# A two-block transformer kernel: four of a head's sixteen expert value rows are weighted and added by VectorE instead of TensorE

## What is computed

```
q = (xt @ w_pq).reshape(T, PEER_HEADS, 2, PEER_QDIM // 2)      # T = 256 tokens, 8 heads
s = einsum('thpd,hpnd->thpn', q, subkeys)
top_s, top_i = lax.top_k(s, 16)                                 # per head and half
...                                                             # 16 best of the 16 x 16 sums
expert = take_along_axis(cand_i, best_pos); gate = softmax(best_s)
act = gelu(einsum('thkd,td->thk', peer_u[expert], x)) * gate    # 16 u rows per head and token
out = einsum('thk,thkd->td', act, peer_v[expert])               # 16 v rows per head and token
x = x + out
```

## Time and profile before

| | |
|---|---|
| timed runs | 1973.23 us median of 3 (1970.73 to 1973.85) |
| profiled execution | span 2142.0 us, 8.6% above the median; no time of its own is given beside the span |
| busy in that span | PE 80%, PE weight loads 51%, DVE 59%, POOL 47%, ACT 29% |
| granted PE clock | 0.88 of full speed, mean |
| DMA | 644.22 MB, mean 301 GB/s; 536.94 MB of it are the 1024 gathers |

### The profile page before, as it was taken

How to read it: one execution, slowest core, us unless ns; L and a number is a source line. 1 busy time by engine, 2 the same in 40 slices (tenths; PEclk the granted TensorE clock), 3 DMA queues, 4 the chain that set the end, 5 groups by cost and what they waited for, 6 DMA issues and landing times. The chain is left out here.

```text
span 2142.0 us, 22067 instructions
## 1 busy us (share of the span) xinstructions
PE 1722.3 (80%) x7643; PEld 1082.0 (51%) x7643; DVE 1254.5 (59%) x2789; ACT 616.9 (29%) x1151; POOL 1008.5 (47%) x1095
## 2 busy tenths in 40 slices
PE   8999999978787686768668999877777867677768
PEld 7998898844443232323224999754442322222323
DVE  6544665885565665566453456685555566476553
ACT  4472644412121111222213455312212111212212
POOL 3021000366666666667672000265666666666663
PEclk9998999989998787878778999898997878788878
DMA  7521553999999999999997756598999999999996
GB/s 253 165 82 60 172 188 116 307 365 341 347 371 373 351 367 383 352 366 368 361 391 241 232 161 197 187 338 332 342 367 375 361 364 370 365 372 370 359 376 240
DMA packets 243719, 644.22 MB, mean 301 GB/s; under 512 B 19541, under 2 KB 105354, under 8 KB 243610
## 3 DMA queue, kind: packets, MB, share of 16 engines
q0 software_dynamic: 147456, 536.94, 66.3%
q1 hardware_dynamic: 96154, 105.88, 15.4%
HBM read 641.69 MB, written 1.05 MB: 300 GB/s over the span
## 5 line engine op out<-in xcount | busy, mean ns | idle before, releaser
L2038 DVE SCALAR_TENSOR_TENSOR ex_uj<-wring,ps 128x1024 f32<-128x1024 f32 x496 | 601.8, 1219 | 409.7 <-DMA wring<-in_peer_u,ex_idx 363.7
L2334 PE MATMUL ps<-ex_v,ex_diag 128*128 128x512 f32 x1328 | 664.6, 647 | 168.4 <-issue 162.6
L2196 POOL DMA_INDIRECT wring<-in_peer_u,ex_idx x496 | 468.6, 945 | 176.1 <-issue 141.4
L2334 PEld LDWEIGHTS ps<-ex_v,ex_diag 128*128 128x128 f32 x1328 | 270.6, 206 | 546.2 <-issue 535.0
L2334 PE MATMUL ps<-value_rows,ex_diag 128*128 128x512 f32 x664 | 360.0, 677 | 135.4 <-issue 134.0
L2211 POOL DMA_INDIRECT ex_v<-in_peer_v,ex_idx x336 | 318.1, 947 | 242.3 <-remote 110.8
L2162 ACT ACTIVATE ex_diag<-ident,ex_weight 128x128 f32<-128x128 f32 x500 | 171.0, 393 | 720.0 <-remote 390.1
L2334 PEld LDWEIGHTS ps<-value_rows,ex_diag 128*128 128x128 f32 x664 | 141.7, 215 | 351.0 <-issue 345.4
L208 DVE TENSOR_TENSOR w_lo<-wring,w_hi 128x1024 fp32r<-128x1024 f32 (+1 forms) x160 | 187.3, 1211 | 108.4 <-ACT w_hi L199 106.1
L2196 POOL DMA_INDIRECT ex_v<-in_peer_u,ex_idx x16 | 16.4, 1023 | 464.1 <-PE ps L283 459.9
L2211 POOL DMA_INDIRECT value_rows<-in_peer_v,ex_idx x172 | 164.2, 955 | 96.3 <-remote 47.2
(11 more groups left out here) (470 smaller groups left out, 2465.0 us busy)
## 6 DMA issues: line engine op xcount, KB each, us to landing
wring<-in_w_in SPq DMA_DIRECT2D x42, 1024.0 KB, 5.4
wring<-in_w_ckv SPq DMA_DIRECT2D x8, 1024.0 KB, 5.3
wring<-in_peer_u,ex_idx POOLq DMA_INDIRECT x496
ex_v<-in_peer_v,ex_idx POOLq DMA_INDIRECT x336
wring<-in_w_mix_out SPq DMA_DIRECT2D x4, 1024.0 KB, 6.6
wring<-in_w_cq SPq DMA_DIRECT2D x4, 1024.0 KB, 5.1
wring<-in_w_co SPq DMA_DIRECT2D x4, 1024.0 KB, 5.2
value_rows<-in_w_pq SPq DMA_DIRECT2D x4, 1024.0 KB, 10.3
```

What stands on the lines that cost most here:

```text
L2038: ve.scalar_tensor_tensor(out=uj[i % 2], in0=u_row(i), scalar=1.0, in1=tokens(g // PH), op0=ALU.mult, op1=ALU.mult, accum_out=hidden[:, g ...
L2196: nc.gpsimd.indirect_dma_start(u_row(i), None, table_u, bass.IndirectOffsetOnAxis(ap=idx[:, g // PH, i % PER_T:i % PER_T + 1], axis=0)).th ...
L2334: last = mm(ps[:, 2 * T + c, :], diag[:, n % DIAGS, :], value_slot(v_slot(j))[:, c * BANK:(c + 1) * BANK], start=j % PER_T == 0, stop=ends)
```

## The change

`VEC_ROWS = {1: 2, 3: 6, 7: 10, 11: 14}`: in heads 0 to 14 of both stages, rows 2, 6, 10 and 14 of a head leave PE and ACT (no diagonal, no matmul). DVE handles them in the next head's loop, behind its u rows 1, 3, 7 and 11 and ahead of the top-k part there: it multiplies the row with its weight column and adds it to the residual tile, with both large operands in SBUF. The last head keeps its six. The slot of such a row is released by `vec_used`, and counts of semaphores are adjusted.

```
+VEC_ROWS = {1: 2, 3: 6, 7: 10, 11: 14}
...
         def on_vector(j):
-            return j >= FIRST_LAST and j - FIRST_LAST in LAST_VEC
+            return j - FIRST_LAST in LAST_VEC if j >= FIRST_LAST else j % TOPK in VEC_ROWS.values()
+
+        def before_on_vector(j):
+            return sum(1 for i in range(j) if on_vector(i))
 
         def on_tensor(j):
-            return j if j < FIRST_LAST else FIRST_LAST + sum(1 for i in range(FIRST_LAST, j) if not on_vector(i))
+            return j - before_on_vector(j)
+
+        VECTOR_ROWS = before_on_vector(ROWS)
+
+        def value_row(v, j):
+
+            T, g = j // PER_T, j // TOPK
+            v_arrived(v, j)
+            n = before_on_vector(j)
+            if n:
+                v.wait_ge(vec_used.sem, vec_used.at(n))
+            nc.vector.scalar_tensor_tensor(out=K.X[:, T, :], in0=value_slot(v_slot(j)), scalar=weight[:, g % 2, j % TOPK:j % TOPK + 1],
+                                           in1=K.X[:, T, :], op0=ALU.mult, op1=ALU.add).then_inc(vec_used.sem, 1)
...
                 if g >= 2:
-                    v.wait_ge(dia.sem, dia.at(TOPK * (g - 1)))
+                    v.wait_ge(dia.sem, dia.at(on_tensor(TOPK * (g - 1))))
...
                                             op0=ALU.mult, op1=ALU.mult, accum_out=hidden[:, g % 2, s:s + 1]).then_inc(u_used.sem, 1)
+                    if g and s in VEC_ROWS:
+                        if s == min(VEC_ROWS):
+                            v.wait_ge(wts.sem, wts.at(g))
+                        value_row(v, (g - 1) * TOPK + VEC_ROWS[s])
...
                 elif v_use(j):
-                    pool.wait_ge(pe_used.sem, pe_used.at(max(m for m in range(j) if slots[m] == n) + 1))
+                    m = max(m for m in range(j) if slots[m] == n)
+                    if on_vector(m):
+                        pool.wait_ge(vec_used.sem, vec_used.at(before_on_vector(m) + 1))
+                    else:
+                        pool.wait_ge(pe_used.sem, pe_used.at(on_tensor(m) + 1))
```

More of the change, by code:

```diff
@@ L1847, in _ @@
                     if n == RAW - 1:
-                        sp.wait_ge(pe_used.sem, pe_used.at(ROWS - len(LAST_VEC)))
-                        sp.wait_ge(vec_used.sem, vec_used.at(len(LAST_VEC)))
+                        sp.wait_ge(pe_used.sem, pe_used.at(ROWS - VECTOR_ROWS))
+                        sp.wait_ge(vec_used.sem, vec_used.at(VECTOR_ROWS))
                     K.load_unit(sp)
@@ L2057, in _ @@
                     first_low(n - len(LAST_VEC) + 3)
[L2058 to L2063, removed]
+                value_row(v, j)
+            v.wait_ge(vec_used.sem, vec_used.at(VECTOR_ROWS))
             add_tokens(NT - 1)
@@ L2170, in _ @@
                 act.wait_ge(pe_used.sem, pe_used.at(on_tensor(more_tensor) + 1))
-                act.wait_ge(vec_used.sem, vec_used.at(LAST_VEC.index(more_vector - FIRST_LAST) + 1))
+                act.wait_ge(vec_used.sem, vec_used.at(before_on_vector(more_vector) + 1))
                 for half in range(2):
@@ L2331, in _ @@
                     pe.wait_ge(s_out.sem, s_out.at(QSTEPS))
-                ends = j == PER_T - 1 or n == ROWS - len(LAST_VEC) - 1
+                ends = j == PER_T - 1 or n == ROWS - VECTOR_ROWS - 1
                 for c in range(2):
@@ L2340, in _ @@
                 first_product()
-        for sig, by in ((tk, TK_EARLY + TK_STEPS * HEADS), (picked, HEADS + 1), (u_used, ROWS), (pe_used, ROWS - len(LAST_VEC)),
-                        (vec_used, len(LAST_VEC)), (dia, ROWS - len(LAST_VEC)), (out_r, NT), (x_ps, NT), (g_exp, HEADS), (g_inv, HEADS),
+        for sig, by in ((tk, TK_EARLY + TK_STEPS * HEADS), (picked, HEADS + 1), (u_used, ROWS), (pe_used, ROWS - VECTOR_ROWS),
+                        (vec_used, VECTOR_ROWS), (dia, ROWS - VECTOR_ROWS), (out_r, NT), (x_ps, NT), (g_exp, HEADS), (g_inv, HEADS),
                         (act_r, HEADS), (wts, HEADS), (ready, HEADS),
```

## The result

The changed kernel takes 1978.79 us (median of 5 runs, 1978.27 to 1982.29) against 1971.98 us of the kernel before in the same comparison (5 runs, 1966.92 to 1973.85). The ratio is 1.0050, with a 95% interval of 1.0033 to 1.0067: slower, by 6.8 us between these medians, and by 9.9 us by the ratio. The forecast said slower, with 1999 us, which is 26 us more, and a range of its own of 1981 to 2029 us, which the result just misses. The sign was right, the size about three times too large, and since most of the loss has a cause that the prediction put at nothing, the right sign was luck.

What follows compares the result with a forecast made beforehand. The prediction took the gathers (POOL or DMA), not PE, as the bound: 1973.2 us, plus 30 us of gather delays, less 4 us of tail, gives 1999 us; own range 1981 to 2029, 8-in-10 range 1957 to 2031.

Steps and rivals of the forecast that it cites:

- What bounds the stage: Expert stages: gathers bound them, by POOL (1.245 us a gather) or DMA (1.276), measured 1.292; PE does not.
- PE is the bound: Rival, both stages: POOL waits for slots PE releases late, so fewer PE rows make it faster, 1960 us; chance 0.26.
- The standstills: Places in the profiled stages where PE, DVE and ACT slow together; read as a recording cost, 168.8 us over the timed run.
- The hold: A DVE value row with two SBUF operands delays a POOL gather starting during it: 0.5 us a row, 2.0 us a head.
- The slack: POOL's beat against DMA's pace, 32 x (1.276 - 1.245) = 1.0 us a head, absorbs part of the gather delays.
- the term of +30 us: Gather delay beyond POOL's slack, 1.0 us in each of 2 x 15 heads, makes the stages 30 us longer.
- DMA hides it: Rival: DMA can't beat 1.292 us a gather, so delays of 0.38 us a row vanish: 1973 us; chance 0.16.
- first come, first served: Explanation of why the gather at 1134.69, 0.02 us behind DVE's start, was not held by DVE's operation.
- The new waits are met: DVE's waits for value rows: row 14 is gathered three row times before its use, so they cost nothing.
- The tail: Matmuls after each stage's last gather: head 14 has four rows fewer on PE, saving 2 us a stage, 4 us total.
- The signs I named: Profile signs: 60 more DVE operations a stage, stretched gathers summing to near 60 us, matmuls from 1992 to some 1510.
- DVE's load: 60 added DVE operations a stage at 1.28 us, 77 us, fit beside the gathers and cost nothing.

Runs made afterwards that it cites:

- second profile of before: The kernel before, unchanged, run and profiled again: span 1965.9 us without the standstills, median 1969.01 us, ratio 1.0001.
- e6: The changed kernel, but head 14's four value rows stay on PE, so only heads 0 to 13 use DVE: 1972.36 us, ratio 1.0015 to before.
- e12: Against the kernel before: eight rows a head on DVE in heads 0 to 13, none in head 14, second operand from PSUM (sum changed): 1972.21 us, ratio 1.0018.
- e10: The changed kernel, but DVE adds rows 10 and 14 of head 14 behind its last u row and the last head's weights: 1971.35 us, ratio 1.0012.
- e7: The changed kernel, but row 14 of head 14 alone goes back to PE: 1971.51 us, ratio 1.0007 to before.
- e8: The changed kernel, but rows 10 and 14 of head 14 go back to PE: 1971.12 us, ratio 1.0009 to before.
- e5: The changed kernel, but only head 14's four value rows are on DVE, those of heads 0 to 13 stay on PE: 1973.55 us, ratio 1.0020.
- e3: The kernel before plus four DVE operations a head with two SBUF inputs, result unused, PE's work unchanged: 1970.72 us, ratio 1.0012.
- e9: Against the kernel before: eight rows a head on DVE in heads 0 to 13, none in head 14, both operands in SBUF: 2035.45 us, ratio 1.0328.

## Why the prediction was right about the sign and wrong about the size

**What bounds the stage: right.** The gathers pace it, and the pace that I inferred from the timed run, 1.292 us, is 658.5 / 511 = 1.289 us in the second profile of before. My 411 GB/s were 409 over the whole stage. PE was not the bound; the rival "PE is the bound" (0.26) is refuted, since a quarter fewer diagonal matmuls on PE made no stage shorter, and e6 to e12 none either. The standstills were rightly set aside, but "a cost of the recording" is not shown: three engines stood, DMA did not, and nothing in any run says why.

**The hold: the mechanism right, one term mis-sized and one left out.** From the pages, all gathers together take 961.6 us before, 994.4 after, 1027.6 with six rows and 1073.3 with eight (e12: 963.5). Divided by 120, 168 and 224 value rows that is 0.27, 0.39 and 0.50 us for a value row. I took 0.5 for four rows, from the assumption that every position in the beat is equally likely; it was 0.27, or 16 us in a stage and not 30.

The slack I set at 1.0 us a head, 15 us in 15 heads. The first stage before runs 658.5 us from first to last gather against 511 x 1.245 = 636 us of beats, so that POOL stands for 22.5 us. But it can't use all of that: with four, six and eight rows the gathers take 661.0, 678.2 and 700.6 us, and the beats and the delays (16, 33 and 56 us) are 652, 669 and 692 of them. Each time about 9 us of standing are left, so that about 14 us, 0.9 us a head, could be filled. The slack was about right.

What I left out is the backlog. Before, the first stage ends 673.8 - 658.5 = 15.3 us behind the start of its last gather, with six and eight rows 9.1 and 9.2 us: transfers that queue let POOL be 6 us later at no cost. So a stage can take some 14 + 6 = 20 us of delays (an estimate from these differences). Four rows' 16 us are below it, and the term of +30 us was about zero. Six rows' 33 us are 13 above it, and the first stage grew by 13.5 us; eight rows' 56 are 36 above it, and it grew by 36.0. The second stage took somewhat more, 24 us: it grew by 9.5 and 30.1 us under 33 and 54 us of delays. The rival "DMA hides it" had the outcome of this term right, with 0.38 us a row and 1.5 us of slack a head.

One reading of the earlier trace rows was wrong. The gather at 1134.69 started 0.02 us behind DVE's operation, so that it did not come first by the record. That it was not held is a fact of the row; "first come, first served" does not follow from it.

**"The new waits are met: row 14 of a head is gathered just ahead of u row 8 of the next head": the step that failed.** It holds for 14 of the 15 heads. In head 14 the order of the gathers is another one, and there row 14 comes after the last u row. The description of the kernel, written with the prediction, says so; the argument did not use it. I cost the wait at nothing; it is 7.7 us long, and it holds up four u rows and the last head's weights, and makes PE's last ten rows the end of the stage: +4.4 and +3.6 us in the two profiled stages, of which PE's lower clock at their start is some 1.7 us each. Against e10 the change is 1978.79 - 1971.35 = 7.4 us slower, with the same work. That is the measured loss but for about 2 us. Taking the late rows away thus gives back 0.38 to 0.43% (e7, e8, e10), adding head 14 alone cost 0.20% (e5), so that by timed medians the late wait is worth between 0.20 and 0.43% of the time, 4 to 8 us.

**The tail: wrong sign.** I took 2 us off for each stage because head 14 has less work on PE. PE was not late there before; in its timeline above it kept step with the landings. With the change it became late, by the wait.

**The signs I named.** Matmuls in the diagonals' groups fell from 1992 to 1512, and 60 value rows in a stage appear, as forecast. The gathers' stretches were to sum to near 60 us; they sum to 33 (994.4 - 961.6). That was the sign, visible in one page, that the hold was about half as large as I had it.

**DVE's load: right.** 77 us in a stage, hidden; e3 has them for 2 us and e12 has nearly twice as many for 3 us.

**What stays open.** All kernels without the late wait lie 1.4 to 3.5 us above before (0.07 to 0.18%), three of the six (e3, e6, e12) with an interval that just excludes zero. The hold isn't needed for it (e12 has none), nor is less work for PE (e3 has all of it). What all six have and before has not is 56 to 112 more DVE operations of 1.2 to 1.3 us in a stage. In their profiles the two stages together are 1.0 to 3.8 us longer than before, so it may lie there; but it is near the limit of what this measurement tells from no change, and its cause stays open. Open is also why the timed loss of the change (0.50%) is larger than that of its two parts together (0.35%).

## What to carry to other kernels

When work moves to an in-order engine, check each of its new waits against the order in which the data is fetched in every phase of the loop, the last one above all, where hand-written orders change: one row of 60 that waits ahead of landed work cost most of the loss, and doing it later on the same engine brought the time back to within 0.12% of before. A lock or a hold costs only what exceeds the slack between the issuer's beat and the transfer's pace, and the backlog in front of it, both measured over the whole stage: four rows a head cost at most 3 us, six cost 21 us and eight 66. And don't size a term on one profiled execution whose span is 8.6% above the timed median: profile again first.

## What the runs showed of the hardware that was not expected

The hold is not a constant of the operation. It was 0.27 us a value row while transfers queued behind one another, and 0.50 us when POOL had become the bound. In the rows of e9 above the value rows start 0.86, 0.39 and 0.40 us ahead of a gather; a likely reason is that DVE, which then works on each row as it lands, keeps step with POOL's issue, so that its value rows fall into a gather's start again and again. This reason is argued, not shown; the eight rows also lie at other places of the head than the four, and no run tells the two apart. One core took 409 GB/s through indirect gathers for 658 us on end, in every run in which POOL kept up; the figure of about 358 GB/s that the Trainium skill ("DMA: Bandwidth & Descriptors", section "Where 436 GB/s comes from") gives for a core's HBM share did not bind here. (The kernel runs on one core; no run has a second one beside it.)
